# Mixing stage of the second block: two block borders removed, products and output blocks reordered

## What is computed

```python
y = jax.nn.gelu(y.reshape(bn, L, SSM_WIDTH))
y = y * jax.nn.sigmoid(y @ w_glu.astype(f32) + b_glu.astype(f32))
y_s = s5_branch(...) @ w_ssm_out[l]
y_m = mlstm_branch(...) @ w_ml_out[l]
mixed = jax.nn.sigmoid(g_s) * y_s + jax.nn.sigmoid(g_m) * y_m
h = h + mixed @ w_out[l]
h = h + peer_ffn(rmsnorm(h, norm2_g[l]), ...)
```

## Time and profile before

| | |
|---|---|
| median of 3 runs | 1791.62 us (1791.55 to 1796.36) |
| the profiled execution | 1792.67 us, of which the trace spans 1790.9 us |
| PE busy | 1672.8 us, 93% of the span |
| DVE, ACT, POOL busy | 1147.1, 800.0, 366.1 us |
| PE's mean granted clock | 0.968 of full speed |

### The profile page before, as it was taken

One profiled execution on the slowest core, in us unless ns is written; L12 is line 12 of the kernel. 1 busy time (PEld: TensorE's weight loads), 2 busy tenths in 40 slices (PEclk: granted clock), 3 DMA queues, 4 the chain that ended last, 5 costly groups with the idle time before them and its releaser, 6 DMA issues. The chain is left out here.

```text
span 1790.9 us, 32793 instructions
## 1 busy us (share of the span) xinstructions
PE 1672.8 (93%) x11200; PEld 1519.7 (85%) x11200; DVE 1147.1 (64%) x2258; ACT 800.0 (45%) x1323; POOL 366.1 (20%) x228
## 2 busy tenths in 40 slices
PE   5979899779999989999989999999999999999997
PEld 4968897669999976777879999999999988888886
DVE  4454412846777674662438998577776577777776
ACT  3442111424555445223335555355555555555554
POOL 0030000403444100224747799100000000000000
PEclk8989999979999999999989999999999999999999
DMA  6503123415555332114434777555555766767663
GB/s 223 187 24 105 48 95 106 141 49 176 187 185 207 127 130 71 36 48 153 145 126 130 243 218 211 188 176 176 176 176 181 238 236 236 238 238 236 234 235 129
DMA packets 92804, 289.44 MB, mean 162 GB/s; under 512 B 10304, under 2 KB 27072, under 8 KB 92352
## 3 DMA queue, kind: packets, MB, share of 16 engines
q1 hardware_dynamic: 92304, 287.61, 48.8%
q10 hardware_dynamic: 432, 0.90, 0.1%
HBM read 270.64 MB, written 17.83 MB: 161 GB/s over the span
## 5 line engine op out<-in xcount | busy, mean ns | idle before, releaser
L259 PE MATMUL psum<-arena_parts 128*128 128x256 f32 (+2 forms) x1664 | 482.7, 290 | 43.6 <-DVE ring_parts L254 11.3
L261 PE MATMUL psum<-arena_parts,ring_parts 128*128 128x256 f32 (+1 forms) x1600 | 454.8, 284 | 0.0
L259 PEld LDWEIGHTS psum<-arena_parts 128*128 128x128 f32 x1664 | 320.6, 193 | 47.9 <-issue 25.5
L2539 DVE TENSOR_TENSOR ring_parts<-ring,arena_parts 128x512 fp32r<-128x512 f32 x418 | 282.9, 691 | 116.4 <-ACT arena_parts L2339 96.2
L261 PEld LDWEIGHTS psum<-arena_parts,ring_parts 128*128 128x128 f32 x1600 | 307.8, 192 | 0.0
L254 POOL TENSOR_TENSOR ring_parts<-ring,arena_parts 128x1024 fp32r<-128x1024 f32 x87 | 229.0, 2650 | 295.4 <-ACT arena_parts L250 278.2
L260 PE MATMUL psum<-h_parts,arena_parts 128*128 128x256 f32 x1024 | 287.7, 281 | 0.0
L230 PE MATMUL psum<-h,ring 128*128 128x256 f32 x896 | 211.5, 396 | 6.0 <-DVE arena L1360 6.0
L230 PEld LDWEIGHTS psum<-h,ring 128*128 128x128 f32 x896 | 176.1, 200 | 34.5 <-issue 9.2
L2308 PE MATMUL psum<-arena_parts,x_parts 128*128 128x512 f32 x512 | 202.1, 395 | 2.7 <-DVE x_parts L2566 2.7
L2309 PE MATMUL psum<-ring_parts,x_parts 128*128 128x512 f32 x512 | 201.0, 393 | 0.0
(11 more groups left out here) (527 smaller groups left out, 2956.1 us busy)
## 6 DMA issues: line engine op xcount, KB each, us to landing
ring<-stream SPq DMA_DIRECT2D x473, 512.0 KB, 3.5
kept<-arena SPq DMA_DIRECT2D x128, 128.0 KB, 2.3
arena<-kept SPq DMA_DIRECT2D x32, 512.0 KB, 4.3
arena<-first SPq DMA_DIRECT2D x1, 2144.0 KB, 7.7
arena<-second SPq DMA_DIRECT2D x1, 1632.0 KB, 6.5
x<-x_t SPq DMA_DIRECT2D x1, 1024.0 KB, 5.7
out<-arena SPq DMA_DIRECT2D x4, 256.0 KB, 2.1
arena<-last ACTq DMA_DIRECT2D x1, 512.0 KB, 3.3
```

Of the source, the lines that this page charges most:

```text
L259: nc.tensor.matmul(dst, stationary[0], moving[0], start=first, stop=False)
L261: return nc.tensor.matmul(dst, stationary[1], moving[0], start=False, stop=last_one)
L2539: v.tensor_tensor(low[:, s, w], ring[:, s, w], expert_high[:, m % 2, w].bitcast(F32), ALU.subtract)\
```

## The change

Three things are changed.

- **Borders.** The two `with nc.Block()` lines between the pieces go. The mixing, the queries and the rest now stand in the Block of the branches, so that each engine goes from one piece's instructions to the next without a barrier. Three waits take the place of what the barriers gave: PE waits on `y_open` (raised by the gelu) before the glu products; query block 0 waits for the parts of x tile by tile; the norm's sum waits on `norm_squares`. ACT's gelu is moved from behind the sixth of the last six gate reads to behind the third.
- **Gate product last in combination one.** The slots of combination 0 are taken in the order 6, 3, 5 and no longer 5, 6, 3: the plain product is its third. The wait for `s5_gated` stands at that product alone. The banks become (3, 4, 2), (5, 6, 7), (2, 3, 4), (5, 6, 7). The load order of the ring stays.
- **Output blocks opened early.** PE waits for `mixed` = 3, runs the k = 0 to 5 products of output blocks 0, 1 and 2 (18 matmuls each, banks 0, 1 and 2), then waits for `mixed` = 4, adds k = 6 and 7 of each (6 matmuls each) and goes on with blocks 3 to 7 as before.

```diff
@@ ScalarE, end of the branches
-                z_reads(act, 6, ACT.Sigmoid)
+                z_reads(act, 3, ACT.Sigmoid)
                 act.wait_ge(y_taken, ONCE + 4)
-                sca.link(a.activation(us[:, :, M:TT], us[:, :, M:TT], ACT.Gelu_apprx_tanh))
+                sca.tell(a.activation(us[:, :, M:TT], us[:, :, M:TT], ACT.Gelu_apprx_tanh), y_open, ONCE + 1)
+                z_reads(act, 3, ACT.Sigmoid)
...
-        combos = ((5, 6, 3), (0, 1, 2), (7, 4, 5), (6, 3, 0))
+            loaded = ((5, 6, 3), (0, 1, 2), (7, 4, 5), (6, 3, 0))
+            combos = ((6, 3, 5),) + loaded[1:]
+            GATE_AT, COMBO_BANKS, OPEN = (2, 0, 0, 0), ((3, 4, 2), (5, 6, 7), (2, 3, 4), (5, 6, 7)), 3
...
-        with nc.Block() as block:
...
-                    if q == 0:
+                    if q == GATE_AT[combo["n"]]:
+                        if combo["n"] == 0:
+                            pe.wait_ge(S("s5_gated"), 1)
                         return gate(q, w, b, i)
...
+                pe.wait_ge(y_open, ONCE + 1)
                 project(pe, (7, 4), (0, 1), 1, gate)
-                pe.wait_ge(S("s5_gated"), 1)
                 pe.wait_ge(S("h_parts"), split["h"] + 1)
                 for n, slots in enumerate(combos):
                     combo["n"] = n
-                    project(pe, slots, ((2, 3, 4), (5, 6, 7))[n % 2], 1, branches)
+                    project(pe, slots, COMBO_BANKS[n], 1, branches)
+                def onto(q, ks):
+                    s, b = cycle[q], q % 4
+                    if ks[0] == 0:
+                        pe.wait_ge(full[s], (pe_at.rounds[s] + 1) * 16)
+                        pe.wait_ge(drained[b], pe_at.banks[b] + q // 4 + 1)
+                    ins = parted(8 + q, bank[b], mixed_high, mixed_low, ks)
+                    if ks[-1] == KT - 1:
+                        ins.then_inc(used[s], 1)
+                pe.wait_ge(S("mixed"), 3)
+                for q in range(OPEN):
+                    onto(q, range(6))
                 pe.wait_ge(S("mixed"), 4)
-                project(pe, cycle, range(4), 1, onto)
+                for q in range(OPEN):
+                    onto(q, range(6, KT))
+                for q in range(OPEN, KT):
+                    onto(q, range(KT))
+                pe_at.advance(cycle, 1, range(4))
...
-                    nc.scalar.activation(qx_squares[:, k, :], x[:, k, :], ACT.Square)
+                    ins = nc.scalar.activation(qx_squares[:, k, :], x[:, k, :], ACT.Square)
+                ins.then_inc(S("norm_squares"), 1)
...
-        with nc.Block() as block:
...
@@ query blocks on TensorE
                         for k in range(KT):
+                            if m == 0:
+                                pe.wait_ge(S("h_parts"), split["h"] - KT + k + 1)
...
                     if n == 0:
+                        pe.wait_ge(S("norm_squares"), normed["squares"])
```

## The result

| | before | changed |
|---|---|---|
| median | 1792.65 us, 4 runs (1791.55 to 1796.36) | 1777.46 us, 4 runs (1774.57 to 1778.71) |
| profiled execution | 1792.67, span 1790.9 | 1774.57, span 1772.8 |
| PE busy | 1672.8 | 1670.4 |
| PE's mean granted clock | 0.968 | 0.975 |

The ratio is 0.9907 with a 95% interval of 0.9890 to 0.9925, 13.4 to 19.7 us saved, 16.7 in the middle. Five further runs of the changed kernel, taken later beside nine of the kernel before, gave 0.9902 (0.9886 to 0.9918). So it is faster by about 0.9%, 3 to 6 us less than the forecast 20.9. The profiled execution of the changed kernel was its shortest of four.

A forecast was written before the change was run, and what follows sets the result against it. PE, inside instructions for 93% of the span, was taken to bound the kernel; 5.1 + 3.9 + 7.2 + 4.7 = 20.9 us off the 1791.62 median gave 1770.7, range 1768.3 to 1776.6.

The forecast's parts named there:

- rival A: Covers too thin: POOL's low parts 2 us later lose 4.2 us, perhaps a 1.7 restart, giving 1776.6; chance 0.15.
- the prediction's own signs: Right if no PE idle above 0.5 us between 820 and 915, clock 1.00; idle near 893 on DVE means thin covers.
- a plain shift: Behind query block 0, other engines start as much earlier as PE does; PE's later idles of 6.9 and 15.0 us unchanged.
- The clock's price: Slow granted clock behind PE's four idles costs 1.68, 1.66, 2.0 and 1.64 us, 7.0 us together.
- Border one: Between branches and mixing, gelu moved: 3.41 us of idle and 1.68 of slow clock go, 5.1 us gained.
- Gate product last: In combination 0 of the mixing: 2.26 us of idle and 1.66 of slow clock go, 3.9 us gained.
- Early output blocks: Between mixing and output blocks: 5.18 us of idle and 2.0 of slow clock go, 7.2 us gained.
- Border two: Ahead of query block 0: 3.31 us of idle and 1.64 of clock go, less a 0.1 to 0.3 stall; 4.7 us.
- rival B: Clock term partly luck: the second idle may already be free of slow clock, gain 19.2 us, 1772.4; chance 0.15.
- C: Rival: idle at both borders is instruction fetching and stays without a barrier; gain 11.1 us, 1780.5; chance 0.06.
- D: Rival, slower: the load ring runs dry, each of eight output blocks waits 4.2 us, 1804.1; chance 0.03.
- No one waits: In the mixing, loads held behind slot 5 cost nothing: reuse takes 7.0 to 7.5 us, shortest gap 18 us.

The follow-up runs named there:

- the joined version: Changed kernel with four output blocks opened early, wait on banks 2 and 3 behind query block 0, ACT's high parts later: stretch 69.23 us, ratio 0.9898.

## Why the prediction was right or wrong

The direction and the mechanism were right: four idles and the slow clock behind them. Against 1791.62 times the ratio, 1775.0, the range of 1768.3 to 1776.6 held; the plain median of 1777.46 lies 0.9 above it. The forecast of 1770.7 was too low by 4 to 7.

That the range held is in part luck. Its upper end stood on rival A, of which 0.5 us came. The largest thing that went missing, 1.6 to 3.1 us behind the stretch, was in no term and in no rival. And by the prediction's own signs not all was right: the idle of 0.97 is above its 0.5, the idle at 893 was its sign for A, and its last sentence ("the forecast of a plain shift was wrong") is what happened. The prediction's sum and its timeline also differ by half a microsecond: the terms make 20.9, the timeline puts the norm's sum 21.4 earlier.

*The clock's price.* 7.0 us for four restarts: borne out. The second trace of before has the slow clock at all four places again, and single restarts cost 1.76 where the gate product was put first and 2.2 where the second barrier was put back.

*Border one, 5.1 us:* the timeline went nearly as laid out. The glu products start with no gap. The second table load stood behind ACT's wait for the fourth gate block and not behind the gelu, so the fourth read came at 837.75, about 0.7 later than laid out, and cost PE nothing. Both loads took 1.28, with 0.02 from the read to the first and 0.01 from the second to the next read. The larger figure of the Trainium skill ("ScalarE: Activation LUTs", What ACT_TABLE_LOAD costs), with the drain, did not show as time here. What was wrong is the reading of the 3.41: I took ACT's gelu plus 0.6 of barrier for it. With the barrier alone put back it is 2.38, of which 1.75 is SP's issuing of loads. Two causes of similar length lay one on the other (2.4 and 2.8 us when each is left alone), and both had to go.

*Gate product last, 3.9 us:* right. The thinnest cover, 0.7 us at POOL's second low part, held; no wait shows at 853. DVE's `y5 * glu` took 2.31 beside POOL where I had carried over 1.23, and was there all the same, 2.4 ahead of its use.

*Early output blocks, 7.2 us:* this term failed by 0.51, in the sentence "I don't take it as shorter or longer". I let the chain from PE's last product to the fourth pair stay 5.18. It was 6.9, since POOL now had a backlog and DVE's last step met a subtraction, 2.77 for 0.69. The durations that I had read belonged to a particular interleaving with POOL, and the change moved that too. In rival A I named this against myself and argued "they did so before, in the durations that I used", which is just what didn't hold.

*Border two, 4.7 us:* 1.1 too much. From PE's last output product to the norm's sum it was 7.77 us before and 4.15 in the changed kernel, 3.6 less. I missed the wait on banks 2 and 3 ahead of query block 0, a line outside the diff that the barrier had made free; and tile 7's low part came 3.6 us behind PE's last product where I had carried over 2.55.

Together the stretch gave 19.3 and 19.8 us in the traces (by A to B) where 20.9 was the sum.

*Behind it a plain shift:* this step failed, by 1.6 in one trace and 3.1 in the other. The work and the idles did shift plainly, 491.58 against 491.60 from B to C in the first traces. The clock behind two unchanged idles did not: free before, paid for in the changed kernel. I had used the idle of 2.18 us that costs nothing as an argument for rival B, that the kernel before might pay less in other executions. The second trace of before refutes that form of it (the clock fell at all four places again). The mechanism, equal idles priced unequally, turned up on the other side, as a cost of the changed kernel. The statement of the Trainium skill ("TensorE: Matmul & The Clock Gate", What's actually happening) that the number of slow matmuls varies from run to run is borne out by the changed kernel's two traces at the first expert block in halves (clock 1.00 and 0.72); at the other places the two traces of a kernel agreed.

19.3 less 1.6 is 17.7, and 19.8 less 3.1 is 16.7. The two ratios say 16.7 and 17.6. What decides whether the clock falls behind an idle of 2.2 or 2.7 us stays open. Among eleven traces with the change or parts of it and no filler it fell behind the longer one in ten, and behind the shorter in five; in the two of before in none. The exception at the longer one is the variant without early blocks. I have no rule that gives this, and don't claim that the change causes it. Open as well is why the piece from C to the end took 370 us in the traces of two variants (the moved bank wait, the joined version), with a steady rate of 4.32 matmuls a microsecond in place of 4.36 at a clock of 1.00. These 3.2 us are more than the joined version won in the stretch.

*Rivals:* A came in part, by its own mechanism, at 0.5 us in the changed kernel and 1.7 in three of the variants. C fell: without barriers nothing remained at the first joint, and what remained at the second went with the bank wait. D fell: no wait on the ring in the stretch. But the held-back loads were not free as I had said ("No one waits"): they bunched ACT's high parts and so gave POOL its backlog, as the variant with the gate product first shows by having neither.

## What to carry to other kernels

A wait taken from before has a cause that may have a twin just behind it: look for what else a barrier waited for (here SP's queue of loads, and a bank wait just outside the diff) before naming one owner of the idle. A duration read beside another engine's work is good only for that interleaving; where a change bunches the other engine's work, bound it by the longest row seen. And judge a part of 1 or 2 us by a stretch between two marks of the trace, not by the whole time, which here moved 3 us between traces for reasons ahead of the change.

## What the runs showed of the hardware

- A subtraction of POOL holds up some of DVE's instructions. A cast of 128x512 took 0.43 us with POOL idle and 2.5 beside a POOL subtraction of 128x1024; a DVE subtraction 0.69 and 2.77; a scalar-tensor-tensor of 128x256 0.48 and 2.3. The longer values are close to one POOL instruction (2.4 to 2.8). DVE's products with one input in PSUM were not held up: in the middle of POOL's run of ten, one of 128x512 took 0.69 and those of 128x256 some 0.4. One wait on POOL shortened DVE's three steps from 6.2 to 1.8 us. POOL is slowed far less: 2.37 us each for the three subtractions with DVE mostly idle, 2.68 in the run of ten.
- SP took 1.75 us to issue four loads of 512 KB. At a barrier this counted, even though nobody needed the loads yet.
- The same idle of PE, 2.7 us, was followed by a clock of 1.00 in both traces of one kernel and 0.72 in both of the other. An idle of 2.26 was followed by 0.50 in both traces of before, while a longer one, 2.38 at the barrier put back alone, was followed by 1.00, and so was that of 0.97. So the length alone doesn't decide at these lengths.
- A float32 product shows as two matmul records, 0.115 us each at 128x128. The 16 matmuls of a plain block are such records, of 8 products in the kernel; a product of fp32r shows as one.
